# A fused decoder layer on one core: another order of experts at the head of the expert stage, and a tail entered without a jump

## The reference, cut to what matters

```python
mix = jnp.concatenate([y_a, y_m], axis=-1) @ w_out          # attention and mLSTM, 512 tokens x 1024
x = _layer_norm(DEEPNORM_ALPHA * x + mix, ln1_g, ln1_b)
ffn = _hierarchical_moe(x, ...)                             # each token: 2 of 32 experts
x = _layer_norm(DEEPNORM_ALPHA * x + ffn, ln2_g, ln2_b)
return x + jax.nn.sigmoid(x @ ple_gate_w) * (p_i @ ple_proj_w)
```

## Time and profile before

| | us |
|---|---|
| median of 3 runs | 667.9 (665.71 to 669.96) |
| the profiled execution, its own time | 671.31 |
| its span in the profile | 669.6 |
| PE busy | 616.2 (92%) |
| DVE, ACT, POOL busy | 364.1, 175.7, 167.3 |
| granted TensorE clock, mean | 0.977 |
| bytes moved | 151.29 MB, 226 GB/s over the span |

### The profile page before, as it was taken

How to read it: one execution, slowest core, us unless ns; L and a number is a source line. 1 busy time by engine, 2 the same in 40 slices (tenths; PEclk the granted TensorE clock), 3 DMA queues, 4 the chain that set the end, 5 groups by cost and what they waited for, 6 DMA issues and landing times.

```text
span 669.6 us, 11512 instructions
## 1 busy us (share of the span) xinstructions
PE 616.2 (92%) x4470; PEld 443.1 (66%) x4470; DVE 364.1 (54%) x862; ACT 175.7 (26%) x347; POOL 167.3 (25%) x181
## 2 busy tenths in 40 slices
PE   8999998999989988999789989989999899849997
PEld 6768978778867866887665545544555555525885
DVE  6779998678777685768561112211211121109946
ACT  4673324253252242402101111111111111125221
POOL 2518362001010010421122333333333333210100
PEclk9999999999999998999899989999999999969999
DMA  7613241014003100197996899999999999975003
GB/s 241 219 34 111 110 183 37 1 36 155 1 0 132 58 0 18 53 369 293 381 362 223 332 416 418 420 418 418 417 420 417 415 420 418 417 309 238 1 1 125
DMA packets 29899, 151.29 MB, mean 226 GB/s; under 512 B 6740, under 2 KB 7020, under 8 KB 15888
## 3 DMA queue, kind: packets, MB, share of 16 engines
q1 hardware_dynamic: 24048, 142.08, 53.3%
q0 software_dynamic: 5792, 8.42, 3.5%
HBM read 147.05 MB, written 13.37 MB: 240 GB/s over the span
## 4 chain that ended last, share of the span: by engine, by line
PE 56%; DVE 14%; issue 5%; DMA 5%; ACT 2%; another core or an unknown queue 1%; POOL 1%; SPq 0%; DVEq 0%; ACTq 0%; POOLq 0%
PE bank L2187 15%; PE bank L2235 8%; PE bank L1824 6%; PE bank L1826 6%; PE bank L1825 6%; DMA y<-in_ple_gate_dram 4%; PE bank L2203 2%; PE bank L2177 2%; PE bank L1968 2%; PE bank L1947 1%; DVE res L1298 1%; PE bank L2227 1%; PE bank L1919 1%; PE bank L1977 1%
## 5 line engine op out<-in xcount | busy, mean ns | idle before, releaser
L1731 DVE COPY rows_x<-bank 128x128 f32<-128x128 f32 (+1 forms) x41 | 11.2, 272 | 182.9 <-PE bank L2227 73.9
L1824 PE MATMUL bank<-w_hi,a_hi 128*128 128x384 f32 (+1 forms) x240 | 88.1, 367 | 0.0
L1826 PE MATMUL bank<-w_hi,a_lo 128*128 128x384 f32 (+1 forms) x240 | 86.6, 361 | 0.0
L1825 PE MATMUL bank<-w_lo,a_hi 128*128 128x384 f32 (+1 forms) x240 | 86.5, 360 | 0.0
L1824 PE MATMUL bank<-a_hi,w_hi 128*128 128x512 f32 (+1 forms) x176 | 69.6, 396 | 2.4 <-DVE a_lo L1480 1.5
L1826 PE MATMUL bank<-a_hi,w_lo 128*128 128x512 f32 (+1 forms) x176 | 67.7, 384 | 0.0
L1825 PE MATMUL bank<-a_lo,w_hi 128*128 128x512 f32 (+1 forms) x176 | 67.6, 384 | 0.0
L789 POOL DMA_INDIRECT pair_dram<-rows_x,row_put x29 | 29.4, 1015 | 113.2 <-ACT rows_x L1060 113.2
L2187 PE MATMUL bank<-raw,rows_x 128*64 128x256 f32 x480 | 56.2, 388 | 0.9 <-DVE rows_x L1702 0.8
L2187 PEld LDWEIGHTS bank<-raw,rows_x 128*64 128x64 f32 x480 | 34.9, 140 | 24.4 <-issue 7.2
L1824 PEld LDWEIGHTS bank<-w_hi,a_hi 128*128 128x128 f32 x240 | 45.3, 189 | 5.2 <-issue 0.3
(11 more groups left out here) (299 smaller groups left out, 1103.3 us busy)
## 6 DMA issues: line engine op xcount, KB each, us to landing
raw<-in_w_exp_dram SPq DMA_DIRECT2D x42, 1024.0 KB
slots<-in_w_exp_dram SPq DMA_DIRECT2D x27, 1024.0 KB
pa<-in_w_exp_dram SPq DMA_DIRECT2D x18, 1024.0 KB
raw<-in_w_in_dram SPq DMA_DIRECT2D x19, 512.0 KB, 3.5
raw<-in_w_wide_dram SPq DMA_DIRECT2D x4, 1536.0 KB, 7.0
rows_x<-in_w_exp_dram SPq DMA_DIRECT2D x6, 1024.0 KB
raw<-in_w_out_dram SPq DMA_DIRECT2D x4, 1024.0 KB, 5.9
raw<-pair_dram SPq DMA_DIRECT2D x8, 512.0 KB, 11.5
```

Of the source, the lines that this page charges most:

```text
L1824: t_.matmul(o, lh, rh, start=first, stop=False)
L1825: t_.matmul(o, lh, rl, start=False, stop=False)
L1826: return t_.matmul(o, ll, rh, start=False, stop=last)
```

## The change

1. `PLACES` has another order: the first expert with one item of 32 seats stands at position 1 and the next at position 4, and the five fixed ones stand at positions 0, 2, 8, 18 and 21 (before: 0, 1, 6, 11 and 15). The counts of each kind stay.
2. At the head of the stage, POOL gathers items 0, 1 and 3, then waits for the rows of the small items and gathers item 2. DVE computes the rows of the other items ahead of the copy of item 0's tokens, the rows of the small ones behind it. PE makes the table of the other items, and 4 more fillers, ahead of turning item 0's tokens. The small table lies in bank 6. PE turns item 1's tokens between the two halves of item 0's gate and up product.
3. `ln2_g` and `ln2_b` are loaded once as 4 rows of 512 (8 KB), early, into `gn_half`, and spread over the partitions by four matmuls with `sel_head` into bank 7 (`spread_norm`) and four copies by ACT (`spread_out`), one pair behind each of four items late in the stage. The two loads of 512 KB go away.
4. The register of the fullest expert is read six items ahead of the end. The tail (`rest`) stands inside the `If`, in the way of the straight path, and again in the `Else` behind the general path. SP keeps its jump.
5. DVE has the splits of pieces 0 and 1 ahead of tile 0's sums, the split of piece 2 behind tile 0's `norm_scale`.

```diff
-PLACES = "FFnsnnFWssnFssnFWsnWnsnsWsnsnsnn"
+PLACES = "FnFsnWssFsnsnWnnWsFnsFnnssnsWsnn"
+FIRST = sorted(range(4), key=lambda i: ITEM[i][1] >= 2 * FIX)
+SPREAD = LAST[AWAY[RINGS - 1]] + 2
+        ln_rows = gn_half[0:4, 0:512]
...
-        def expert_blocks(eng, run, fill):
-            run(0, 0, 0)
-            fullest = eng.value_load(most[0:1, 0:1], min_val=0, max_val=SEQ)
-            with eng.If(fullest > P):
...
+        def fullest_expert(eng):
+            return eng.value_load(most[0:1, 0:1], min_val=0, max_val=SEQ)
+
+        def general_blocks(eng, run, fill):
+            eng.sem_inc(s_full, 1)
+            eng.wait_ge(s_full, 5)
+            fill(PADDED - ITEMS)
+            eng.sem_inc(s_full, 1)
+            eng.wait_ge(s_full, 10)
+            with eng.Fori(1, SEQ // SEATS + 1) as b:
+                run(b, b * NE + PADDED - NE, b * NE - NE)
+
+        def expert_blocks(eng, run, fill, rest):
+            fullest = run(0, 0, 0)
+            with eng.If(fullest < P + 1):
+                rest()
+            with eng.Else():
+                general_blocks(eng, run, fill)
+                rest()
...
# SP
                 store(0)
+                sp.dma_start(ln_rows, d["ln2_gb"]).then_inc(s_lnw2, 16)
                 store(1)
...
-                sp.wait_ge(s_dn, LAST[AWAY[RINGS - 1]] + 1)
-                sp.dma_start(ln_g, d["ln2_g"].partition_broadcast(P)).then_inc(s_lnw2, 16)
-                sp.dma_start(ln_b, d["ln2_b"].partition_broadcast(P)).then_inc(s_lnw2, 16)
...
# POOL
-                for i in range(4):
-                    gather(i, column[i])
+                for i in FIRST if isinstance(b, int) else range(4):
+                    if isinstance(b, int) and column[i] >= FIXED:
+                        pool.wait_ge(s_rows, 7)
+                    (gather_small if is_small[i] else gather)(i, column[i])
...
# ACT
+            def spread_out(r):
+                act.wait_ge(s_pp, r + 1)
+                a.activation(pa[:, 4096 + r * 512:4096 + (r + 1) * 512], bank[7][:, :], ACT.Copy).then_inc(s_pev, 1)
...
+                        if 0 <= T - SPREAD < 4:
+                            spread_out(T - SPREAD)
...
# DVE
             values(found[:, :, 0:REST], REST)
+            dve.wait_ge(s_tabp, 2)
+            rows(FIXED, ITEMS)
             tokens(0, 0)
             dve.wait_ge(s_tabp, 3)
-            rows(FIXED, ITEMS)
             small_rows()
...
+                        if T == ITEMS - 6:
+                            fullest = fullest_expert(dve)
...
-                    for q in range(3):
-                        split_gate(q)
...
+            def rest():
+                split_gate(0)
+                split_gate(1)
+                for t in range(NT):
+                    expert_sum(t, 0)
...
+                    if t == 0:
+                        dve.wait_ge(s_pev, 4)
+                    norm_centre(t, s_ln2)
+                    norm_scale(t, s_ln2, s_rs2)
+                    if t == 0:
+                        split_gate(2)
+                    if t == 1:
+                        split_gate(3)
...
# PE
-            def gate_up(T, par, full, s):
+            def gate_up(T, par, full, s, q0=0, q1=2):
...
+            def spread_norm(r):
+                if r:
+                    pe.wait_ge(s_pev, r)
+                else:
+                    pe.wait_ge(s_lnw2, 16)
+                t_.matmul(bank[7][:, :], sel_head[:, r, :], ln_rows, start=True, stop=True).then_inc(s_pp, 1)
...
                     idle_products(bank[3], a_hi[:, 2, :], 24)
+                    tables(TB_FIXED + 3, REST)
+                    idle_products(bank[3], a_hi[:, 2, :], 4)
                     turn_tokens(0, 0)
-                    tables(TB_FIXED + 3, REST)
                     small_tables()
...
+                        else:
+                            gate_up(T, T % 2, landed(n), SLOT[n], 0, 1)
+                            turn_tokens(T + 1, (T + 1) % 4)
+                            gate_up(T, T % 2, landed(n), SLOT[n], 1, 2)
...
+                        if 0 <= T - SPREAD < 4:
+                            spread_norm(T - SPREAD)
```

More of the change, by code:

```diff
@@ L62 @@
 FIRST_NARROW = IS_SMALL.index(True)
[L63 removed]
+assert FIRST_REST < 4 and FIRST_NARROW < 4
 RINGS = 6
@@ L620, in fill @@
                 pass
-            expert_blocks(sp, run, fill)
+            fullest = run(0, 0, 0)
+            with sp.If(fullest > P):
+                general_blocks(sp, run, fill)
             sp.wait_ge(s_gu, 2 * ITEMS)
@@ L829, in fill @@
                     pool.wait_ge(s_put[s], 4 * PADDED)
-            expert_blocks(pool, run, fill)
-            for t in range(NT):
-                inverse(t, s_ve2, s_rs2)
+            def rest():
+                for t in range(NT):
+                    inverse(t, s_ve2, s_rs2)
+            expert_blocks(pool, run, fill, rest)
         @block.scalar
@@ L1087, in fill @@
                 act.sem_inc(s_outa, count)
[L1089 to L1098, removed]
-                             turned_2[u % 4][:, :].rearrange("p (k c) -> p k c", k=4), ACT.Copy).then_inc(s_x2hi, 1)
@@ L1116, in _, with rest, turned_high, sigmoid @@
-            sigmoid(2 * NT - 2)
-            sigmoid(2 * NT - 1)
+            def rest():
+                for q in range(3):
+                    round_gate(q)
+                for u in range(2 * NT):
+                    ple_out(u)
+                act.wait_ge(s_glo, 2)
+                def turned_high(u):
+                    t, half = u // 2, u % 2
+                    act.wait_ge(s_x2t, u + 1)
+                    a.activation(a_hi[:, 4 * half:4 * half + 4, t * P:(t + 1) * P],
+                                 turned_2[u % 4][:, :].rearrange("p (k c) -> p k c", k=4), ACT.Copy).then_inc(s_x2hi, 1)
+                def sigmoid(u):
+                    act.wait_ge(s_gt, u + 1)
+                    if u >= 2 * NT - 2:
+                        act.wait_ge(s_mix, 4)
+                    a.activation(sig[:, u // 2, (u % 2) * 512:(u % 2 + 1) * 512], gate_bank[u % 4][:, :], ACT.Sigmoid)\
+                        .then_inc(s_sig, 1)
+                for t in range(NT):
+                    turned_high(2 * t)
+                    turned_high(2 * t + 1)
+                    if t == 0:
+                        round_gate(3)
+                    else:
+                        sigmoid(2 * t - 2)
+                        sigmoid(2 * t - 1)
+                sigmoid(2 * NT - 2)
+                sigmoid(2 * NT - 1)
@@ L1119, in _ @@
+            expert_blocks(act, run, fill, rest)
         @block.vector
@@ L1818, in _ @@
+            expert_blocks(dve, run, fill, rest)
         @block.tensor
@@ L2327, in layout @@
+            expert_blocks(pe, run, fill, rest)
 def layout(x, p, w_in, b_igate, b_fgate, conv_w, conv_b, gn_w, w_out, ln1_g, ln1_b, router_group_w, router_group_b,
```

202 lines of the change are left out of this document (88 added, 114 removed).

## The result

The kernel after takes 664.29 us (median of 8 runs, 660.80 to 667.13), the kernel before 668.00 on the same chip: ratio 0.9937 [0.9916, 0.9958]. Measured again beside the experiments it was 664.42 for 668.18, ratio 0.9951 [0.9925, 0.9976]. So the gain is about 4 us, half of the 8.1 forecast (659.8), inside the range of 655.5 to 666.0. The two profiled executions are further apart, 671.31 and 665.39; where that comes from is one of the findings.

A forecast was written before the change was run, and what follows sets the result against it. It took the weight stream as the bound, PE close behind, PE alone in the last 47 us. Stream, scatter, pair loads and splits put the first gate product at 610.1 for 618.19: 8.1 us gained, 659.8, range 655.5 to 666.0.

The forecast's parts named there:

- Stream: Weight transfers up to the tail: the third gate piece lands at 595.15 instead of 604.35, by 5 plus 4.2 us.
- The order: Head of the stage: new expert order releases ring loads sooner, winning 5 us of stream, bounds 2.5 to 8.0.
- the norm vectors: SP's queue ahead of the gate pieces: dropping two 0.5 MB loads wins 4.2 us, bounds 2.5 and 4.2.
- Item 0: First item on PE: full clock saves 1.74 us, the hidden token copy 0.71; together 2.45, bounds 0.7 and 2.45.
- Spreading: Late in the stage on PE: four matmuls spreading the norm vectors cost 0.47 us each, 1.9 us in all.
- Last waits: PE's last two waits, 1.33 and 1.02 us ahead of down products, were for weights that now come sooner: 2.35 won.
- the ring runs short: Rival, positions 9 to 17: later fixed experts leave PE without weights for 13 us; 5.0 slower, 672.9; chance 0.07.
- Scatter 6.16 us, then 3.5: Start of the tail: the last scatter lands 6.16 us after issue, at 594.6, the pair loads 3.5 later, at 598.1.
- Branch: Start of the tail: without the jump PE starts 6.0 us sooner, which is worth nothing in itself.
- The jump at the end: Rival, end of tail: a 6.03 us jump over the `Else`; 0 likely, at most 3.5 us, 663.3; chance 0.06.
- Splits: Tail on DVE: the third split's 2.29 us, saved ahead of tile 0's sum, is paid behind its scale.
- the head doesn't reach the end: Rival: clock stays low, PE's lag swallows the lead, last down product at 591.3; gain 4.0, 663.9; chance 0.17.

The follow-up runs named there:

- e3: Kernel after with the old order of experts and POOL's two table waits back in their place; ratio 1.0005 to the kernel before.
- e4: Kernel after with the norm vectors again loaded by two 0.5 MB loads ahead of the gate pieces, no spreading on PE; ratio 0.9957 to the kernel before.
- e6: Kernel before with only the new form of the branch (tail inside the `If` on all engines but SP); ratio 1.0022 to the kernel before.
- e9: Kernel after with item 0, the tables and the turning of item 1's tokens as before, new order kept; ratio 0.9953 to the kernel before.
- e1: Kernel after with all but 8 of the 512 columns left out of each of the four spreading matmuls; ratio 0.9928 to the kernel before.
- e10: Kernel after with the third gate piece's split on POOL, 1 filler for 10, norm vectors loaded behind tile 0's pair, no spreading; ratio 0.9959 to the kernel before.
- e2: Kernel after with the old branch: a test that is jumped over, the tail behind it; ratio 1.0050 to the kernel before.
- e5: Kernel after measured once more, unchanged; ratio 0.9951 to the kernel before.
- e7: Kernel after with the third gate piece's split behind tile 0's two low parts, and 1 filler for 10; ratio 0.9941 to the kernel before.
- e8: As e7, with the third gate piece loaded behind tile 0's pair loads; ratio 0.9949 to the kernel before.
- e11: Kernel after with norm vectors loaded behind tile 0's pair, 1 filler for 10, the third gate piece loaded behind tile 1's pair; ratio 0.9944 to the kernel before.
- e12: Kernel after with the third split ahead of tile 0's sum again and 6 fillers for 10; ratio 0.9946 to the kernel before.

## Why the prediction was right in kind and wrong by half

*Stream: right, in part by luck.* The third gate piece was forecast at 595.15, 253.7 behind the gather; it landed at 253.8. The order was put at 5 us and is at most 4.2 to 4.4 (e3), the norm vectors at 4.2 and are 3.0 to 3.2 (e4), nearer to the bytes' 2.5 than to the queue's 4.2. Both terms were too large, and what is missing from the measured 9.0 was made up by the slow item 0 of the profiled execution of before, the next point. Against e6, where the piece landed at 260.4, the gain is 6.6.

*Item 0: the step that failed.* "So I take the full clock: 5.36 - 3.62 = 1.74". The 5.36 belongs to one execution: the other two traces with the old head, e6 and e9, have 3.67 and no lower clock there. And it reached the end of the stage: in e6, with the same head but item 0 at 3.67, the third gate piece landed at 260.4 instead of 262.8 and the first sum came at 264.6 instead of 267.0. So 2.4 us of the forecast gain were none: an execution of before like that of e6 doesn't lose them. "Carried over, the median becomes 659.8" was the same mistake again, since the 3.4 us by which the profiled execution lay above the median very likely held the loss that the change was credited with removing. With e6 for the kernel before, the account closes: first sum 264.6 to 259.0 or 259.9, that is 4.7 to 5.6, less 1.8 for the split that is now behind the scale (4.06 to the first product for 2.24) makes 2.9 to 3.8; the medians say 3.7. This rests on single traces; how often an execution of before has the slow item 0 is not known.

*Spreading: mis-sized.* "Four matmuls, at the 14.21 / 30 = 0.47 us": the row counts records, and an fp32 product of 512 columns leaves two of them: `embed` is 16 matmuls (not 32, as said of the kernel before) with 32 records, so it costs 13.99 / 16 = 0.87 a product. A spread took 1.12, and the short items' products behind the last two 2.36 and 2.41 instead of 1.95: 4 x 1.12 + 0.41 + 0.46 = 5.3 us for 1.9. It reached the end with 0.6 to 1.5 us (e1), for it stood in part in time that PE would else have idled (e4), and a later scatter lands faster.

*Last waits (2.35 won): mostly right.* The weights are no longer late there, but 0.33 of each wait is the chain of hidden values and stays, so 1.7 are won. The rival "the ring runs short" got no support: at the longest waits of the kernel after the weights had landed 5.4 to 21.6 us before.

*PE's way to the last down product.* From item 1's end it took 6.3 us more than before: 7.8 more of work, 1.6 less of idle time. Of the work 5.3 are the spreading and 1.7 the clock, which fell twice (at 446.1 and 470.0) where it fell once in the kernel before (at 389.7); 0.8 is not assigned. The forecast had the last down product 245.7 behind the gather; it came at 251.4 to 252.1.

*Scatter 6.16 us, then 3.5: right only while the stream runs.* Last down product to pair issue was 7.4 in the kernel before and in e6, 7.0 in e3 and e4, 5.6 in e1, 6.6 in e10, and 3.8 to 4.6 in the kernel after, e2, e5, e7, e8, e9, e11 and e12, where it had ended or nearly so. So PE's 5.6 us behind the forecast cost only 2.3 at the first sum (600.40 for 598.1): a scatter that is issued later lands faster. It also works the other way: an earlier PE wins little, as e1 shows.

*Branch: right alone, wrong in the sum.* "Worth nothing in itself" holds in the kernel before (e6). Here it is worth 7 us (e2): embedding and fillers end at 609.7, behind the scale at 607.9, so PE has no room left. The jump at the end exists, 4.21 us on PE at 654.5, but it ends at 658.7, before DVE's last sum at 660.8; that rival's price was 0. The Trainium skill (Runtime: NRT & Kernel Launch, Instruction fetch mechanics) has a taken branch stall when its target isn't in the pages already fetched. PE's three jumps agree, at 3.53, 4.21 and 6.03 us; the jumps of DVE, ACT and POOL, under 0.1 us each, show no such stall, so the prediction's "both engines would stall there" did not come true for DVE.

*Splits: paid behind, right.* Scale to first product was forecast as 4.53 and is 4.06; e12 and e7 show that neither place wins.

*The rival "the head doesn't reach the end"* gave 663.9 and was nearest, with 0.17, by luck. Its PE is nearly right (last down product at 591.3, measured 592.8); its reason is not: the clock was full in the head, there was only little to win by it, and PE's lag came from the spreading and from a slow clock later. It has the first product at 614.2, the forecast at 610.1, the profile at 611.9.

What stays open: the sum of the parts. Taking out the order costs 4 us, taking out the branch 7, and the norm vectors or the head 0 to 1, while all of it together wins 4; the terms stand in for each other, and intervals of 1.5 us either way don't settle each to less than that. What makes the waits of 1.8 to 2.3 us behind some `n` is not known; the old order has them too (e3, four of 1.89 to 2.26). Nor do I know what made the gather of the profiled execution of before land late.

## What to carry to other kernels

Before a slow stretch is credited to a change, ask whether it is the code's or the execution's: a second trace with the same head (e6) shows item 0 at 3.67. Before a wait is called one for weights, look when they landed. Where two chains end within 2 us of each other (stream and PE here, then DVE and PE in the tail), add up each to the end and take the later; a gain on one is worth at most their distance. And an idle gap on PE can cost twice, by its length and by the clock behind it: those of 4 to 6 us in the tail did each time (e2, e6, e10), those of 1.8 to 2.3 us in the stage only sometimes (at 445 and 469, but not at 535). So take fillers out only where no wait takes their place.

## What the hardware showed that I had not expected

A scatter to DRAM followed by loads of what it wrote took 3.8 us from the last product with the queues empty, 7.4 under a full stream. A jump on PE's sequencer took 3.5 to 6.0 us, on DVE, ACT and POOL under 0.1. DVE's first sum of 128 x 1024 lost some 0.75 us to 1.0 us of a POOL subtraction beside it (e10, one profile).
